# Encoder layer with a top-4-of-32 expert stage: halves of the gate/up loads, 128 stationary columns, bias on row groups

## The chip, the core and the metric

The kernel runs on one core of a Trainium2 chip. Five engines work beside each other: TensorE (PE, matrix products; PEld is its loading of the stationary operand), VectorE (DVE), ScalarE (ACT), GpSimd (POOL) and SyncE (SP), which issues most transfers. The sixteen DMA engines move data between the chip's memory and the core's buffer SBUF; TensorE writes into the eight banks of PSUM, each 128 partitions by 512 fp32. The metric is the time of one execution on the device in microseconds; the number compared is the median of several.

## What is computed

One layer of an encoder on 512 rows of 1024: three kinds of attention, a gated merge, and then an expert stage, on which the change lies. Cut to that:

```python
logits = ht @ w_router + b_router            # 512 rows, 32 experts
top_v, top_i = lax.top_k(logits, 4); gate = softmax(top_v)
# each of the 4 x 512 (row, expert) pairs goes to a block of its expert
def expert_block(args):
    xb, e = args
    gu = xb @ w_gu[e] + b_gu[e]              # 1024 x 2048, fp32
    g = jnp.minimum(gu[:, :D_EXPERT], SWIGLU_LIMIT)
    lin = jnp.clip(gu[:, D_EXPERT:], -SWIGLU_LIMIT, SWIGLU_LIMIT)
    act = g * jax.nn.sigmoid(SWIGLU_ALPHA * g) * (lin + 1.0)
    return act @ w_down[e] + b_down[e]       # 1024 x 1024, fp32
x = x + sum of gate * expert_block rows;  return rmsnorm(x, norm_final)
```

## The kernel before

The first 440 us hold the attention, the merge and the router, as 18 weight units of 512 columns. The rest is the expert stage. It works through jobs: a job is up to 96 rows (SLOTS) of one expert. There are 32 jobs with these inputs.

Products are near fp32. Each operand is split into a high part that TensorE takes in one pass (fp32r) and a low part, the rest. A product is high x high, high x low and low x high.

**Parts.** The weights of a job come as 12 parts of 1 MB, each 128 partitions by 2048 fp32: eight parts of the first matrix (gate/up, one chunk k of 128 input features each) and four of the second (down, two chunks each). A gate/up part has rows of 8192 bytes, a down part two rows of 4096 bytes per partition. They land in 12 slots `a_w` in turn. ScalarE copies part m into one of 8 slots `h_w` (the high part, `moe_high`), eight parts ahead of TensorE; VectorE writes the low part `l_w` over `a_w` (`moe_low`), seven ahead. TensorE finishes a part and adds 1 to `gemm_ps`; this frees the `h_w` slot for ScalarE and the `a_w` slot for SyncE, which then issues the load of the part twelve later (`load_gu` L591, `load_dn` L594, each one DMA that adds 16 to the slot's semaphore `part_in`). `wait_raw` waits for it.

**TensorE.** `gate_up` (L1731) first puts the bias into banks 0 to 3: four matmuls (L1735) with the stationary operand `expert_gu`, 96 x 96, and the moving operand `bias_gu`, the biases of all 32 experts in bf16 three times, as high, middle and low part on 3 x 32 partitions. Then for each part k: eight matmuls (L1743) with `xt_hi` and `xt_lo` (the job's rows, transposed, chunk k, 128 x 96) on `h_w`, and four (L1746) with `xt_hi` on `l_w`. Results stand on PSUM partitions 0 to 95. `down` (L1750) does the same with `at_hi`, `at_lo` into banks 4 and 5 (L1761, L1766). Eight transposes (`turn`, L1467) stand after part 1 of gate/up (the activated rows of the job before) and after part 0 of down (the rows of a later job). In the loop a pass has gate/up of job j+1 and then down of job j. The order on each engine is the order of the code, and engines meet at semaphores.

At the end, `down_biases` (L1810, its matmuls L1814) uses the bias of down on groups of 32 partitions, in plain fp32.

**Others.** GpSimd prepares `bias_gu` (L940 to L960), gathers a job's rows (`xg`, indirect DMA L971) and adds finished rows into `x_rows` (L976). ScalarE writes `expert_gu` for each job by broadcasting a column of `job_hot_b` (`name_gu`).

Of the kernel before, what the change touches and what calls it, by code (L numbers as in the profile page):

```python
# [102 lines left out]
def encoder_kernel(nc, x, mem, norm_mix, w_in, q_norm_a, k_norm_a, sink_b, norm_mem, w_mem_kv,  # L103
# [3 lines left out]
    with ctx:  # L107
# [40 lines left out]
        bias_f = sb("bias_f", [96, D], F32, 188 * KIB)  # L148
# [49 lines left out]
        bias_gu = sb("bias_gu", [96, 2 * D], BF16, 202 * KIB)  # L198
# [27 lines left out]
        blocks_end = small("blocks_end", [P, 3, N_EXP], F32)  # L226
        blocks_start = small("blocks_start", [P, 3, N_EXP], F32)
        job_ge = small("job_ge", [96, NJ], F32)
        job_lt = small("job_lt", [96, NJ], F32)
        job_hot = small("job_hot", [96, NJ], F32)  # L230
# [26 lines left out]
        at_hi = sb("at_hi", [P, KD, SLOTS], F32R, 174 * KIB)  # L257
        at_lo = sb("at_lo", [P, KD, SLOTS], F32R, 177 * KIB)
# [16 lines left out]
        job_hot_b = small("job_hot_b", [96, NJ], BF16)  # L275
        expert_gu = small("expert_gu", [96, SLOTS], BF16)
# [253 lines left out]
        def wait_raw(eng, i, m):  # L530
            eng.wait_ge(part_in[m % A_SLOTS], i * 32 + 16 * (m // A_SLOTS + 1))
# [13 lines left out]
        def _(sp):  # L545
# [44 lines left out]
            def load_gu(e, m, k):  # L590
                sp.dma_start(a_w[m % A_SLOTS][:], wgu[e, :, k, :]).then_inc(part_in[m % A_SLOTS], 16)  # L591
# [63 lines left out]
        def _(act):  # L655
# [157 lines left out]
            def moe_high(i, m):  # L813
                wait_raw(act, i, m)
# [22 lines left out]
            def name_gu(j):  # L837

                nc.scalar.activation(expert_gu[:], job_hot_b[:, bass.ds(j, 1)].to_broadcast([96, SLOTS]), ACT.Copy).then_inc(expert_gu_ready, 1)

            def take_xt(j):
                act.wait_ge(x_ps, j + 1)
                nc.scalar.activation(xt_hi[:].rearrange("p (h k) m -> p h (k m)", h=2), of_two_banks(6), ACT.Copy).then_inc(xt_hi_done, 1)

            def take_act(j):
                act.wait_ge(at_ps, j + 1)
                nc.scalar.activation(at_hi[:].rearrange("p (h k) m -> p h (k m)", h=2), of_two_banks(6), ACT.Copy).then_inc(at_hi_done, 1)
# [60 lines left out]
            for p in range(KD):  # L908
# [5 lines left out]
                moe_high(pairs_but_one, stream(0, p) + H_LEAD)  # L914
# [19 lines left out]
        def _(pool):  # L934
# [6 lines left out]
            bias_pieces = [(bias_gu[:, 0:D], b_gate_up[0][:, 0:D]), (bias_gu[:, D:2 * D], b_gate_up[0][:, D:2 * D])]  # L941
            pool.wait_ge(y_ps, STEPS)
            for n, (part, bias) in enumerate(bias_pieces):
                for g in range(3):
                    pool.dma_start(bias_f[N_EXP * g:N_EXP * (g + 1), :], bias).then_inc(bias_in, 16)
                pool.wait_ge(bias_in, 48 * (n + 1))

                def to_parts(rows):
                    step.link(nc.gpsimd.tensor_copy(part[rows, :], bias_f[rows, :]))

                def take_off(rows):
                    step.link(nc.gpsimd.tensor_tensor(bias_f[rows, :], bias_f[rows, :], part[rows, :], ALU.subtract))

                to_parts(slice(0, 96))
                for lo in (32, 64):
                    take_off(slice(lo, lo + 32))
                    to_parts(slice(lo, lo + 32))
                take_off(slice(64, 96))
                to_parts(slice(64, 96))
# [32 lines left out]
            step.link(nc.gpsimd.memset(expert_gu[:], 0.0))  # L992
            for g in range(3):
                nc.gpsimd.memset(expert_gu[N_EXP * g:N_EXP * g + 1, :], 1.0).then_inc(first_expert, 1)
            pool.wait_ge(first_expert, 3)
# [49 lines left out]
        def _(dve):  # L1045
# [227 lines left out]
            for g in range(3):  # L1273
                step.inc(nc.vector.tensor_tensor_scan(blocks_end[:, g, :], ones[:, 0:N_EXP], blocks[:], 0.0, ALU.mult, ALU.add))
            dve.wait_ge(dve_chain, step.n)
            for g in range(3):
# [4 lines left out]
            dve.wait_ge(blocks_ready, 3)  # L1281
# [4 lines left out]
            step.inc(nc.vector.tensor_tensor(job_ge[:], counter[0:96, 0:NJ], ps[0:96, 1, P:P + NJ], ALU.is_ge))  # L1286
            step.link(nc.vector.tensor_tensor(job_lt[:], counter[0:96, 0:NJ], ps[0:96, 1, 0:NJ], ALU.is_lt))
# [39 lines left out]
            def low_xt(j):  # L1327
                dve.wait_ge(xt_hi_done, j + 1)
                nc.vector.tensor_tensor(xt_lo[:].rearrange("p (h k) m -> p h (k m)", h=2), ps[:, 6:8, 0:4 * SLOTS],  # L1329
                                        xt_hi[:].bitcast(F32).rearrange("p (h k) m -> p h (k m)", h=2), ALU.subtract).then_inc(xt_lo_done, 1)  # L1330

            def low_act(j):
                dve.wait_ge(at_hi_done, j + 1)
                nc.vector.tensor_tensor(at_lo[:].rearrange("p (h k) m -> p h (k m)", h=2), ps[:, 6:8, 0:4 * SLOTS],
                                        at_hi[:].bitcast(F32).rearrange("p (h k) m -> p h (k m)", h=2), ALU.subtract).then_inc(at_lo_done, 1)
# [101 lines left out]
        def _(pe):  # L1437
# [264 lines left out]
            pe.wait_ge(blocks_ready, 3)  # L1702
# [27 lines left out]

            def gate_up(i, j, m0, between):  # L1731
# [129 lines left out]
```

## Time and profile before

| | us |
|---|---|
| median of 3 runs (1602.7 to 1605.66) | 1604.47 |
| the profiled execution | 1600.28 |
| its span | 1598.4 |
| PE busy in the span | 1566.0 |
| DVE busy | 1283.4 |
| ACT busy | 1084.7 |
| POOL busy | 432.0 |

The profile is of one execution, and its times are from the start of its span. Busy time of TensorE overstates it, since matmuls are pipelined and their ends are modelled; the starts are better to count with. "Chain" is the work that ended last, followed back from the end. The DMA share is the mean busy share of 16 engines and can pass 1 where packets overlap. 466.97 MB were moved in all.

### The profile page before, as it was taken

Reading aid. Unit: us, or ns where it says so; the run is one execution under the profiler, and the core shown is the slowest. Engines: PE = TensorE matmul, PEld = TensorE weight load, DVE = VectorE, ACT = ScalarE, POOL = GpSimd, SP = SyncE. Lnnn points to the kernel's source line nnn. Section 1 sums busy time; section 2 is a strip of 40 time slices with the busy share of each in tenths; the row PEclk is TensorE's granted clock in tenths of the full one; section 3 lists DMA queues with packets and bytes.
Section 4 is the critical chain, followed back from the end, with each engine's and each line's share of the span. In section 5 each row is a group of like instructions: output and inputs, shape, how many; then the busy total and the mean of one; then the engine's idle time right before and its main releaser. Section 6 shows DMA issues by size and latency. Waiting matters only on the chain.

```text
span 1598.4 us, 21810 instructions
## 1 busy us (share of the span) xinstructions
PE 1566.0 (98%) x7654; PEld 1139.1 (71%) x7654; DVE 1283.4 (80%) x1019; ACT 1084.7 (68%) x999; POOL 432.0 (27%) x265
## 2 busy tenths in 40 slices
PE   8999999999899999999999999999999999999997
PEld 7866688888766777777777777777777777777774
DVE  3768734337699989999898899998988999999984
ACT  6368723224477778777777787777777877777772
POOL 0000260000033622324432222344332223443220
PEclk9999999999999999999999999999999999999999
DMA  7310022337399999999999999999999999999983
GB/s 270 111 59 21 11 86 84 128 119 290 122 381 346 365 367 379 368 369 376 358 369 370 370 381 368 372 369 360 367 369 372 363 377 368 368 363 373 375 298 125
DMA packets 102566, 466.97 MB, mean 292 GB/s; under 512 B 13289, under 2 KB 13825, under 8 KB 69729
## 3 DMA queue, kind: packets, MB, share of 16 engines
q1 hardware_dynamic: 94416, 448.71, 73.5%
q0 software_dynamic: 7776, 17.68, 5.2%
q8 instruction: 24, 0.39, 0.1%
q10 hardware_dynamic: 336, 0.08, 0.0%
q14 instruction: 14, 0.11, 0.0%
HBM read 456.82 MB, written 19.27 MB: 298 GB/s over the span
## 4 chain that ended last, share of the span: by engine, by line
PE 91%; DVE 6%; issue 1%; DMA 1%; ACT 0%; POOL 0%; DVEq 0%; ACTq 0%; POOLq 0%
PE ps L1743 28%; PE ps L1761 14%; PE ps L1746 14%; PE ps L1766 7%; PE ps L1440 6%; PE ps L1442 6%; PE ps L1441 6%; PE ps L1467 4%; DVE l_w L1190 2%; PE ps L1735 2%; PE ps L1593 1%; DVE head_max L1119 1%; PE ps L1549 1%; DVE probs L1137 1%; PE ps L1476 0%
## 5 line engine op out<-in xcount | busy, mean ns | idle before, releaser
L1190 DVE TENSOR_TENSOR l_w<-a_w,h_w 128x2048 fp32r<-128x2048 f32 x384 | 865.4, 2290 | 31.0 <-ACT h_w L817 29.1
L817 ACT ACTIVATE h_w<-a_w 128x2048 fp32r<-128x2048 f32 x384 | 731.1, 1914 | 234.5 <-PE ps L1746 169.2
L965 POOL TENSOR_TENSOR mark_sb<-ones 1x1 f32<-1x1 f32 x93 | 245.9, 2644 | 718.6 <-ACT y_sb L865 708.5
L1743 PE MATMUL ps<-h_w,xt_hi 128*96 128x512 f32 x1024 | 286.7, 401 | 2.3 <-DVE xt_lo L1329 2.3
L1743 PE MATMUL ps<-h_w,xt_lo 128*96 128x512 f32 x1024 | 278.3, 393 | 0.0
L1746 PE MATMUL ps<-l_w,xt_hi 128*96 128x512 f32 x1024 | 277.9, 393 | 0.0
L1743 PEld LDWEIGHTS ps<-h_w,xt_lo 128*96 128x96 f32 x1024 | 165.6, 162 | 71.5
L1746 PEld LDWEIGHTS ps<-l_w,xt_hi 128*96 128x96 f32 x1024 | 165.2, 161 | 71.1
L1743 PEld LDWEIGHTS ps<-h_w,xt_hi 128*96 128x96 f32 x1024 | 163.3, 162 | 70.6 <-ACT h_w L817 1.7
L1761 PE MATMUL ps<-h_w,at_hi 128*96 128x512 f32 x512 | 162.1, 398 | 0.2 <-issue 0.2
L1761 PE MATMUL ps<-h_w,at_lo 128*96 128x512 f32 x512 | 159.5, 392 | 0.0
L486 DVE TENSOR_TENSOR w_low<-w_raw,w_high 128x2048 fp32r<-128x2048 f32 (+2 forms) x36 | 69.0, 1953 | 112.0 <-ACT w_high L478 112.0
L1766 PE MATMUL ps<-l_w,at_hi 128*96 128x512 f32 x512 | 139.0, 393 | 0.0
L1440 PE MATMUL ps<-w_high,h_hi 128*128 128x512 f32 x352 | 138.1, 392 | 0.6 <-DVE mem_lo L1065 0.5
L1442 PE MATMUL ps<-w_high,h_lo 128*128 128x512 f32 x352 | 137.1, 390 | 0.0
L1441 PE MATMUL ps<-w_low,h_hi 128*128 128x512 f32 x352 | 137.0, 389 | 0.0
L1761 PEld LDWEIGHTS ps<-h_w,at_lo 128*96 128x96 f32 x512 | 82.6, 161 | 36.1
L1766 PEld LDWEIGHTS ps<-l_w,at_hi 128*96 128x96 f32 x512 | 82.6, 161 | 35.9
L1761 PEld LDWEIGHTS ps<-h_w,at_hi 128*96 128x96 f32 x512 | 80.2, 162 | 32.1 <-issue 1.0
L971 POOL DMA_INDIRECT xg<-h_rows,gather_row x32 | 88.0, 2749 | 7.1 <-issue 5.4
L785 ACT ACTIVATE gate_sb<-ps,row_rstd 128x512 f32<-128x512 f32 x24 | 16.6, 690 | 105.7 <-PE ps L1442 105.7
L1440 PEld LDWEIGHTS ps<-w_high,h_hi 128*128 128x128 f32 x352 | 66.1, 188 | 15.1 <-DVE mem_lo L1065 0.8
(247 smaller groups left out, 1555.6 us busy)
## 6 DMA issues: line engine op xcount, KB each, us to landing
a_w<-in_w_gate_up SPq DMA_DIRECT2D x256, 1024.0 KB, 7.0
a_w<-in_w_down SPq DMA_DIRECT2D x128, 1024.0 KB, 6.6
w_raw<-in_w_in SPq DMA_DIRECT2D x8, 2048.0 KB, 8.0
w_raw<-in_w_out SPq DMA_DIRECT2D x2, 2048.0 KB, 7.6
w_raw<-in_w_in SPq DMA_DIRECT2D x2, 1024.0 KB, 7.8
x_sb<-in_x SPq DMA_DIRECT2D x8, 256.0 KB, 7.3
w_raw<-in_w_mem_kv SPq DMA_DIRECT2D x1, 2048.0 KB, 11.2
x<-in_x SPq DMA_DIRECT2D x4, 512.0 KB, 5.2
```

Of the source, the lines that this page charges most:

```text
L486: nc.vector.tensor_tensor(wl[u % 2][:, a * COLS:b * COLS], raw[u % 2][:, a * COLS:b * COLS], wh[u % 2][:, a * COLS:b * COLS].bitcast(F32), ...
L817: nc.scalar.activation(h_w[m % H_SLOTS][:], a_w[m % A_SLOTS][:], ACT.Copy).then_inc(wh_done, 1)
L965: nc.gpsimd.tensor_tensor(mark_sb[:], ones[0:1, 0:1], ones[0:1, 0:1], ALU.mult).then_inc(marked, 1)
L971: nc.gpsimd.indirect_dma_start(out=xg[s][:], out_offset=None, in_=h2_rows, in_offset=bass.IndirectOffsetOnAxis(ap=rows, axis=0), bounds_ch ...
L1190: nc.vector.tensor_tensor(l_w[m % A_SLOTS][:], a_w[m % A_SLOTS][:], h_w[m % H_SLOTS][:].bitcast(F32), ALU.subtract).then_inc(wl_done, 1)
L1440: nc.tensor.matmul(bank, hi, w_hi, start=start, stop=False)
L1441: nc.tensor.matmul(bank, hi, w_lo, start=False, stop=False)
L1442: return nc.tensor.matmul(bank, lo, w_hi, start=False, stop=stop)
L1743: nc.tensor.matmul(ps[0:SLOTS, n, :], x_part[:, k, :], w_h[:, n * COLS:(n + 1) * COLS], start=False, stop=False)
L1746: last = nc.tensor.matmul(ps[0:SLOTS, n, :], xt_hi[:, k, :], w_l[:, n * COLS:(n + 1) * COLS], start=False, stop=k == KD - 1)
L1761: nc.tensor.matmul(ps[0:SLOTS, 4 + n, :], a_part[:, 2 * q + k, :], w_h[:, (2 * k + n) * COLS:(2 * k + n + 1) * COLS], start=q == 0 and k = ...
L1766: last = nc.tensor.matmul(ps[0:SLOTS, 4 + n, :], at_hi[:, 2 * q + k, :], w_l[:, (2 * k + n) * COLS:(2 * k + n + 1) * COLS], start=False, s ...
```

## The change

- `load_gu` issues two DMAs per gate/up part, one for each half of the columns (rows of 4096 bytes). Both add 16 to the same semaphore; `landings` counts 32 for a gate/up part and 16 for a down part, and `wait_raw` waits for the sum.
- The stationary operand has 128 columns instead of 96. `xt` and `at_both` hold high and low part in a row, and `chunk` takes 128 columns from the start of a chunk of 96: the last 32 belong to the next chunk, and PSUM partitions 96 to 127 get values that nobody reads. The last chunk of the low part has nothing behind it and keeps 96 columns.
- The bias is split in two fp32r parts, `bias_hi` and `bias_lo`, with columns n x 512 to n x 512 + 511 on partitions 32 n to 32 n + 31. Each of the eight matmuls takes one group of 32 partitions and writes one bank, the four of `bias_hi` first. `expert_gu` is 128 x 128 in fp32r.
- GpSimd's preparation and some router tables follow these shapes (four copies instead of three).

```diff
-        bias_gu = sb("bias_gu", [96, 2 * D], BF16, 202 * KIB)
+        bias_hi = sb("bias_hi", [P, COLS], F32R, 202 * KIB)
+        bias_lo = sb("bias_lo", [P, COLS], F32R, 204 * KIB)
...
-        xt_hi = sb("xt_hi", [P, KD, SLOTS], F32R, 160 * KIB)
-        xt_lo = sb("xt_lo", [P, KD, SLOTS], F32R, 163 * KIB)
+        xt = sb("xt", [P, 2, KD * SLOTS], F32R, 160 * KIB)
+        xt_hi, xt_lo = (xt[:, n, :].rearrange("p (k m) -> p k m", k=KD) for n in range(2))
...
-        job_hot_b = small("job_hot_b", [96, NJ], BF16)
-        expert_gu = small("expert_gu", [96, SLOTS], BF16)
+        job_hot_b = small("job_hot_b", [P, NJ], F32)
+        expert_gu = small("expert_gu", [P, P], F32R)
...
+        def landings(m):
+
+            of_gate_up = m < KD or (m - KD) % PARTS < KD
+            return 32 if of_gate_up else 16
+
+        def wait_raw(eng, i, m, last_down=False):
+            once = sum(landings(n) for n in range(m % A_SLOTS, m, A_SLOTS)) + (16 if last_down else landings(m))
+            again = 0 if isinstance(i, int) else 2 * landings(m)
+            eng.wait_ge(part_in[m % A_SLOTS], i * again + once)
...
             def load_gu(e, m, k):
-                sp.dma_start(a_w[m % A_SLOTS][:], wgu[e, :, k, :]).then_inc(part_in[m % A_SLOTS], 16)
+                for n in range(2):
+                    half = slice(n * D, (n + 1) * D)
+                    sp.dma_start(a_w[m % A_SLOTS][:, half], wgu[e, :, k, half]).then_inc(part_in[m % A_SLOTS], 16)
...
-            bias_pieces = [(bias_gu[:, 0:D], b_gate_up[0][:, 0:D]), (bias_gu[:, D:2 * D], b_gate_up[0][:, D:2 * D])]
             pool.wait_ge(y_ps, STEPS)
...
+            for n in range(4):
+                pool.dma_start(bias_f[N_EXP * n:N_EXP * (n + 1), :], b_gate_up[0][:, n * COLS:(n + 1) * COLS]).then_inc(bias_in, 16)
+            pool.wait_ge(bias_in, 64)
+            step.link(nc.gpsimd.tensor_copy(bias_hi[:], bias_f[:]))
+            step.link(nc.gpsimd.tensor_tensor(bias_lo[:], bias_f[:], bias_hi[:].bitcast(F32), ALU.subtract))
...
-            step.link(nc.gpsimd.memset(expert_gu[:], 0.0))
-            for g in range(3):
-                nc.gpsimd.memset(expert_gu[N_EXP * g:N_EXP * g + 1, :], 1.0).then_inc(first_expert, 1)
-            pool.wait_ge(first_expert, 3)
+            step.link(nc.gpsimd.memset(expert_gu[:].bitcast(F32), 0.0))
+            for n in range(4):
+                nc.gpsimd.memset(expert_gu[N_EXP * n:N_EXP * n + 1, :].bitcast(F32), 1.0).then_inc(first_expert, 1)
+            pool.wait_ge(first_expert, 4)
...
+            def chunk(both, part, k):
+
+                w = SLOTS if part and k == KD - 1 else P
+                at = (part * KD + k) * SLOTS
+                return both[:].rearrange("p a m -> p (a m)")[:, at:at + w], w
+
             def gate_up(i, j, m0, between):

                 pe.wait_ge(expert_gu_ready, j + 1)
-                for n in range(4):
-                    nc.tensor.matmul(ps[0:SLOTS, n, :], expert_gu[:], bias_gu[:, n * COLS:(n + 1) * COLS], start=True, stop=False)
+                for part in (bias_hi, bias_lo):
+                    for n in range(4):
+                        rows = slice(N_EXP * n, N_EXP * (n + 1))
+                        nc.tensor.matmul(ps[:, n, :], expert_gu[rows, :], part[rows, :], start=part is bias_hi, stop=False)
...
-                    for x_part in (xt_hi, xt_lo):
+                    for part in range(2):
+                        x_part, rows = chunk(xt, part, k)
                         for n in range(4):
-                            nc.tensor.matmul(ps[0:SLOTS, n, :], x_part[:, k, :], w_h[:, n * COLS:(n + 1) * COLS], start=False, stop=False)
+                            nc.tensor.matmul(ps[0:rows, n, :], x_part, w_h[:, n * COLS:(n + 1) * COLS], start=False, stop=False)
```

On TensorE, in the loop, at the start of a gate/up product. `bias_gu`, `bias_hi` and `bias_lo` are moving operands, and `h_w`, `l_w` with a number are slots. Before:

```order
L1735 MATMUL ps<-bias_gu,expert_gu 96x512 [waits expert_gu_ready]
L1735 MATMUL ps<-bias_gu,expert_gu 96x512 x3
L534 ISA [waits xt_lo_done]
L1743 MATMUL ps<-h_w_176,xt_hi 96x512 [waits wh_done]
L1743 MATMUL ps<-h_w_176,xt_hi 96x512 x3
L1743 MATMUL ps<-h_w_176,xt_lo 96x512 x4
L1746 MATMUL ps<-l_w_172,xt_hi 96x512 [waits wl_done]
```

Now, at the same place:

```order
L1740 MATMUL ps<-bias_hi,expert_gu 128x512 [waits expert_gu_ready]
L1740 MATMUL ps<-bias_hi,expert_gu 128x512 x3
L1740 MATMUL ps<-bias_lo,expert_gu 128x512 x4
L542 ISA [waits xt_lo_done]
L1749 MATMUL ps<-h_w_177,xt 128x512 [waits wh_done]
L1749 MATMUL ps<-h_w_177,xt 128x512 x7
L1752 MATMUL ps<-l_w_173,xt 128x512 [waits wl_done]
```

Four more matmuls stand ahead of the wait for the low part of the rows; the others keep their places, and their results have 128 rows instead of 96.

On SyncE, the loads of the first gate/up part of the loop and the wait of the next. Before:

```order
L591 ISA [waits gemm_ps]
L591 DMA a_w_160<-in_w_gate_up 128x2048
L540 REGISTER_ALU
L591 ISA [waits gemm_ps]
L591 DMA a_w_161<-in_w_gate_up 128x2048
```

Now:

```order
L601 ISA [waits gemm_ps]
L601 DMA a_w_161<-in_w_gate_up 128x1024
L601 ISA
L601 DMA a_w_161<-in_w_gate_up 128x1024
L548 REGISTER_ALU
L601 ISA [waits gemm_ps]
L601 DMA a_w_162<-in_w_gate_up 128x1024
```

Each wait on `gemm_ps` now has two transfers of half the size behind it (the slot's number differs by one because the tiles are counted anew).

## Rows read from the trace of the kernel before

**Rows 1.** The page: the chain that ended last, by engine.

```profile
PE 91%; DVE 6%; issue 1%; DMA 1%; ACT 0%; POOL 0%; DVEq 0%; ACTq 0%; POOLq 0%
```

**Rows 2.** Chain, one job (928.91 to 964.37): start us, us, what.

```profile
928.91 0.87 PE ps L1735 x4
929.78 1.84 PE ps L1743 x8
931.62 0.92 PE ps L1746 x4
...
955.38 0.66 PE ps L1467 x8
...
964.37 0.87 PE ps L1735 x4
```

**Rows 3.** Chain, where TensorE takes it over, and after the last down product.

```profile
504.03 2.08 PE ps L1743 x8
...
1580.61 1.91 PE ps L1814 x4
```

**Rows 4.** Waits of the SyncE queue, 520 to 1520: us in total, times, longest.

```profile
SPq L591 <- PE ps L1746: 500.0, 226, 2.8
```

**Rows 5.** Window of one job: us, busy (x) of PE, PEld, DVE, ACT, POOL; PEclk, DMA share, GB/s.

```profile
929.37:964.82 35.45, 35.45 (x165) 25.01 (x164) 32.06 (x18) 27.59 (x20) 11.82 (x7) 1.00 1.00 372
```

**Rows 6.** Chain, 128-column matmuls of the projections, first and last of 142.

```profile
254.99 0.23 PE ps L1441
...
286.95 0.23 PE ps L1441
```

**Rows 7.** Window without DMA in the last job, and chain there, 96 columns.

```profile
1561.51:1566.80 5.29, 5.29 (x29) 3.86 (x28) 2.04 (x1) 0.00 (x0) 0.00 (x0) 1.00 0.01 2
...
1560.97 1.85 PE ps L1761 x8
1562.83 0.93 PE ps L1766 x4
```

**Rows 8.** Chain, 128 columns, second, 11th and 20th matmul after transposes.

```profile
21.94 0.23 PE ps L1441
...
24.03 0.23 PE ps L1441
...
26.07 0.23 PE ps L1441
```

**Rows 9.** The page, part 5: loads of 96 and of 128 stationary columns.

```profile
L1743 PEld LDWEIGHTS ps<-h_w,xt_lo 128*96 128x96 f32 x1024 | 165.6, 162 | 71.5
...
L1440 PEld LDWEIGHTS ps<-w_high,h_hi 128*128 128x128 f32 x352 | 66.1, 188 | 15.1 <-DVE mem_lo L1065 0.8
```

**Rows 10.** Chain at the down bias, then PE's timeline at the scores.

```profile
1567.20 1.92 PE ps L1814 x8
...
1569.27 2.09 PE ps L1761 x8
...
112.99 1.13 PE L1549 MATMUL ps<-k_t,q_t 64*128 64x512 f32 x4
114.05 1.09 PE L1467 MATMUL ps<-ident,probs 128*128 128x128 f32 x8
```

**Rows 11.** SyncE's issues of gate/up parts, 504 to 1540: ns min/median/max.

```profile
L591 SPq DMA_DIRECT2D a_w<-in_w_gate_up x232: 333/333/349, 507.2 to 1520.1; - x116
```

**Rows 12.** Windows with 2048-byte rows and with 8192-byte rows, columns as in rows 5.

```profile
10.00:15.00 5.00, 5.00 (x38) 4.74 (x37) 2.73 (x4) 2.37 (x4) 0.00 (x0) 1.00 1.05 395
...
445.00:450.00 5.00, 5.00 (x25) 3.54 (x24) 5.00 (x2) 3.52 (x2) 1.40 (x1) 1.00 1.01 426
```

**Rows 13.** Landings of gate/up loads issued at 908.9 and at 932.7.

```profile
DMA to landing us min/median/max: 8.1/8.1/8.1
...
DMA to landing us min/median/max: 4.7/4.7/4.7
```

**Rows 14.** Timeline of GpSimd before the first gather.

```profile
427.32 0.62 POOL L994 MEMSET expert_gu<- 1x96 bf16 x3
```

More of the change, by code:

```diff
@@ L251, in encoder_kernel @@
         h_w = [sb(f"h_w{i}", [P, 2 * D], F32R, at * KIB) for i, at in enumerate((0, 8, 16, 24, 128, 136, 112, 120))]
[L254 to L255 removed]
+        xt = sb("xt", [P, 2, KD * SLOTS], F32R, 160 * KIB)
+        xt_hi, xt_lo = (xt[:, n, :].rearrange("p (k m) -> p k m", k=KD) for n in range(2))
         xg = [sb(f"xg{i}", [SLOTS, D], F32, (166 + 4 * i) * KIB) for i in range(2)]
[L257 to L258 removed]
+        at_both = sb("at_both", [P, 2, KD * SLOTS], F32R, 174 * KIB)
+        at_hi, at_lo = (at_both[:, n, :].rearrange("p (k m) -> p k m", k=KD) for n in range(2))
         sg_sb = sb("sg_sb", [SLOTS, D], F32, 180 * KIB)
@@ L1272, in _ @@
             step.link(nc.vector.tensor_scalar(blocks[:, 0:1], blocks[:, 0:1], 1.0, None, ALU.max))
-            for g in range(3):
+            for g in range(TB):
                 step.inc(nc.vector.tensor_tensor_scan(blocks_end[:, g, :], ones[:, 0:N_EXP], blocks[:], 0.0, ALU.mult, ALU.add))
             dve.wait_ge(dve_chain, step.n)
-            for g in range(3):
+            for g in range(TB):
                 nc.vector.tensor_tensor(blocks_start[:, g, :], blocks_end[:, g, :], blocks[:], ALU.subtract).then_inc(blocks_ready, 1)
             step.inc(nc.vector.tensor_scalar(job_table[0:1, 1, 1:2], blocks_end[0:1, 0, N_EXP - 1:N_EXP], 0.5, -0.75, ALU.mult, ALU.add))
-            dve.wait_ge(blocks_ready, 3)
+            dve.wait_ge(blocks_ready, TB)
             step.link(nc.vector.scalar_tensor_tensor(out=place[:], in0=blocks_start[:, 0:1, :].to_broadcast([P, TB, N_EXP]), scalar=float(SLOTS),
@@ L1740, in gate_up @@
                     wait_high(pe, i, m)
-                    for x_part in (xt_hi, xt_lo):
+                    for part in range(2):
+                        x_part, rows = chunk(xt, part, k)
                         for n in range(4):
-                            nc.tensor.matmul(ps[0:SLOTS, n, :], x_part[:, k, :], w_h[:, n * COLS:(n + 1) * COLS], start=False, stop=False)
+                            nc.tensor.matmul(ps[0:rows, n, :], x_part, w_h[:, n * COLS:(n + 1) * COLS], start=False, stop=False)
                     wait_low(pe, i, m)
                     for n in range(4):
-                        last = nc.tensor.matmul(ps[0:SLOTS, n, :], xt_hi[:, k, :], w_l[:, n * COLS:(n + 1) * COLS], start=False, stop=k == KD - 1)
+                        last = nc.tensor.matmul(ps[:, n, :], chunk(xt, 0, k)[0], w_l[:, n * COLS:(n + 1) * COLS], start=False, stop=k == KD - 1)
                     last.then_inc(gemm_ps, 1)
@@ L1758, in down @@
                     for k in range(2):
-                        for a_part in (at_hi, at_lo):
+                        for part in range(2):
+                            a_part, rows = chunk(at_both, part, 2 * q + k)
                             for n in range(2):
-                                nc.tensor.matmul(ps[0:SLOTS, 4 + n, :], a_part[:, 2 * q + k, :], w_h[:, (2 * k + n) * COLS:(2 * k + n + 1) * COLS],
-                                                 start=q == 0 and k == 0 and a_part is at_hi, stop=False)
+                                nc.tensor.matmul(ps[0:rows, 4 + n, :], a_part, w_h[:, (2 * k + n) * COLS:(2 * k + n + 1) * COLS],
+                                                 start=q == 0 and k == 0 and part == 0, stop=False)
                     wait_low(pe, i, m)
@@ L1765, in down @@
                         for n in range(2):
-                            last = nc.tensor.matmul(ps[0:SLOTS, 4 + n, :], at_hi[:, 2 * q + k, :], w_l[:, (2 * k + n) * COLS:(2 * k + n + 1) * COLS],
+                            last = nc.tensor.matmul(ps[:, 4 + n, :], chunk(at_both, 0, 2 * q + k)[0], w_l[:, (2 * k + n) * COLS:(2 * k + n + 1) * COLS],
                                                     start=False, stop=q == DN_PARTS - 1 and k == 1)
```

54 lines of the change are left out of this document (19 added, 35 removed).

## The prediction

> **What bounds the kernel now.** I read the page first, then the chain of waits over one job of the expert stage, then the waits of the SyncE queue, then the windows. The chain that ended last is 91% TensorE [rows 1], but 98% busy of TensorE would not prove it, since ends of matmuls are modelled. The chain shows it: from one bias (L1735) to the next, 928.91 to 964.37 us, every piece is TensorE and none is a wait; a job takes 35.46 us, and a part of the weights (8 matmuls with h_w, 4 with l_w) 1.84 + 0.92 us [rows 2]. TensorE takes the chain over from VectorE at 504.03 us [rows 3]. Before that point the stage is still catching up behind VectorE's splits, so what TensorE saves before 504 us gains nothing. From there to the end of the last down product (1580.61 us) lie 30 gate/up products and 31 down products. The SyncE queue waits for it, 500.0 us in all, for free slots [rows 4]. In one job VectorE is busy 32.06 of 35.45 us and ScalarE 27.59, but the DMA engines' share is 1.00 at 372 GB/s [rows 5]. So there is about 3.4 us of room on VectorE, and perhaps none on DMA.
>
> The sum is made against the profiled execution, 1600.28 us with a span of 1598.4; the median of the runs shown is 1604.47, 0.26% above. I subtract the saving from the median.
>
> **Part 1, 128 columns in the stationary operand.** The count of the main matmuls stays: 96 in a gate/up product, 48 in a down product. What counts is the step from start to start. Before, a job has 35.46 - 0.87 (bias) - 2 x 0.66 (transposes) = 33.27 us for 144 matmuls, 231.0 ns each [rows 2]. The projections have the same matmul with 128 columns: from 254.99 to 286.95 us lie 141 of them, 226.7 ns each [rows 6]. The difference is 4.4 ns. DMA traffic is not its cause: in the last job, with a DMA share of 0.01, 12 matmuls of 96 columns still took 2.78 us, 231.7 ns each [rows 7]. But 128 columns do not give 226.7 at once. After the transposes at 20 to 21.5 us, the nine matmuls from 21.94 to 24.03 us took 232 ns each, and only the next nine 226.7 [rows 8]. It is as if the pipeline has to settle after a break. A job has five breaks: two groups of transposes, the bias, and the two places where 96 columns remain (the low part of chunk 7, 4 matmuls in gate/up and 2 in down, which must not read past the tile). I take nine unsettled matmuls after each, 45, plus the 6 themselves: 93 of 144 are settled, 93 x 4.4 = 0.41 us per job. If none of it settles the gain is 0; if all 138 do, 0.60 us.
>
> Loading 128 columns takes 188 ns against 162 [rows 9]. Inside a run of matmuls this is hidden, since 188 is under the step of 227; after a break the first load is exposed, 26 ns at three breaks, 0.08 us per job.
>
> The Trainium skill, "TensorE: Matmul & The Clock Gate", section "LDWEIGHTS (loading the stationary operand)", speaks against this change: a load costs its columns / 1.2 ns, so 32 columns more cost 27 ns. The trace agrees on the size (26 ns). Were each load exposed, the job would be 144 x 27 ns = 3.9 us slower; the rows of the projections show that it is hidden.
>
> **Part 2, the bias.** Removed: 4 matmuls in bf16 over 96 rows, 0.87 us in the chain [rows 2]. Added: 8 over 32 rows each, on four different row groups and four banks, high parts first. The nearest row is the down bias (L1814), also 32 rows by 128 columns between full-width matmuls. There 8 passes over two row groups take 1.92 us, and 4 passes on a single row group 1.91 us, so two row groups do run side by side [rows 3, 10]. A pass of this plain fp32 product is about 0.43 us: at the scores (L1549, 64 rows) two rounds of two passes take 1.06 us with all around them [rows 10]. After its end at 1569.12 us come 0.16 us of nothing up to 1569.27, and then eight matmuls that take 2.09 us where 1.85 is usual. Four rounds of 0.43 are 1.71, so entering and leaving the 32-row form cost 1.92 + 0.16 + 0.24 - 1.71 = 0.61 us. The scores give less: 1.06 us for two rounds, 0.21 us over. An fp32r pass streams once where plain fp32 streams at half that rate: about 0.21 us. With four groups side by side the bias costs 2 x 0.21 + 0.61 = 1.03 us, +0.16 per job; with the overhead of the scores 0.63, -0.24. I take +0.10, nearer to L1814, whose form and surroundings are those of the new bias. Four groups at once is not shown by any row; if only two overlap, it is 0.42 us more per job, and if none do, 1.26.
>
> The Trainium skill, "TensorEngine Tiling", section "Key Properties", states that a change of tiling mode drains TensorE. The 0.61 us of L1814 agrees with it; the page gives no price.
>
> **Part 3, two transfers of half rows.** Same bytes; 8 of a job's 12 loads become 16 of 512 KB. SyncE spends 0.33 us to issue one [rows 11]; two in a part's 2.76 us fit, and both sit behind the same wait on its queue, so nothing else is held up by more than 0.33 us. ScalarE now waits for both halves, and the second is issued 0.33 us later. On the DMA engines the price is the row. With 8192-byte rows a window moved 426 GB/s at a share of 1.01, with 2048-byte rows 395 at 1.05 [rows 12]: 311 and 87 ns per row and engine, so on a straight line 162 for 4096 bytes, 13 ns more per 8192. A job has 8 loads of 8 such rows on each of 16 engines: 64 x 13 = 0.83 us of DMA time. What hides it is slack between issue and need. A load is issued when TensorE frees its slot and is needed by ScalarE four parts later, 11.1 us. A landing took 8.1 us at its worst in a job and 4.7 at the best [rows 13], so the queue does run nearly empty once per job. I charge 0.
>
> **Part 4, the rest.** GpSimd's preparation of the bias gets shorter (4 loads and 2 operations for 6 and 12), far off the chain. Before the first gather it sets one row more and a larger tile: three rows took 0.62 us [rows 14], so about +0.25 us once, on the chain. One scan, one subtraction and a wider copy of the expert's column vanish beside TensorE.
>
> **Sum.** Per job -0.41 + 0.08 + 0.10 = -0.23 us; 30 jobs, -6.9; the last down product has no bias, -0.1; start +0.25. About -6.8 us: profiled 1593.5, median 1597.7, 0.4% faster.
>
> **Rivals.**
> A. The settled step comes at once everywhere and leaving the row groups is cheap: -0.60 - 0.1 per job, -21 us, 1583.5. For: stretches of over a hundred matmuls at 226.7. Against: the slow nine after a break. More likely half of it, about 1590.
> B. DMA becomes the bound. If the share of 1.00 is real work, a job needs 35.46 + 0.83 = 36.3 us and the whole run is 30 x 0.83 = 25 us slower, 1629; it decides as soon as the landings pass 11 us and ScalarE waits for a_w. Against: landings fall to 4.7 us in each job, and a share above 1 (1.05 in one window) shows that the share overstates. With part of it, 0.3 us per job over now, 1613. This is the case on the other side.
> The Trainium skill, "DMA: Bandwidth & Descriptors", section "Rules for kernel authors", asks for at least 1 MiB per DMA, so it would side with B; no run here shows 512 KB transfers in a row yet.
> C. The row groups overlap only in twos: -0.23 + 0.42 = +0.19 per job, +6, 1610; with none, +1.03 per job, +31, 1635.
> D. The split does not do what it says: alternating banks or waits inside each part, not the columns, give 231 ns. Then 0 + 0.08 + 0.10 per job, +5.6, 1610.
>
> **How the numbers follow.** Differences within 0.2% (3.2 us) are about what a measurement of this kernel can tell from no change. Forecast 0.47 (0.40 faster, 0.07 same; own range 1592 to 1602); A 0.14, faster; B 0.13 (0.03 faster, 0.03 same, 0.07 slower); C 0.14 (0.04 same, 0.10 slower); D 0.12 (0.04 same, 0.08 slower). Faster 0.57, same 0.18, slower 0.25. The range runs from the half of A to the milder B: 1587 to 1613.
>
> **What would show it.** Right: in the chain of a job the eight matmuls with h_w take 1.81 to 1.82 us in most parts instead of 1.84, the bias about 1.0 us, the job 35.2, landings of the halves stay under 10 us and no ScalarE wait on a_w appears. Wrong: parts still at 1.84 (D), the bias at 1.4 or more (C), a wait of ScalarE or VectorE for the transfer of a_w and a job over 35.5 (B), a job under 34.9 (A).

## The result

| | before | after |
|---|---|---|
| median of 7 runs each | 1603.7 (1602.42 to 1605.66) | 1608.63 (1605.8 to 1611.17) |
| the profiled execution, its span | 1600.28, 1598.4 | 1605.8, 1603.9 |

The ratio is 1.003, 95% interval 1.0019 to 1.0042: slower by 0.3%. The forecast was 1597.7, faster; the time lies inside the range (1587 to 1613), but on the other side of no change.

The page of the changed kernel: busy time, the chain by engine, and the gate/up loads (KB each, median us to landing).

```profile
PE 1570.6 (98%) x7782; PEld 1248.9 (78%) x7782; DVE 1278.7 (80%) x1021; ACT 1085.7 (68%) x999; POOL 394.6 (25%) x252
...
PE 92%; DVE 5%; issue 1%; DMA 1%; ACT 0%; POOL 0%; DVEq 0%; ACTq 0%; POOLq 0%
...
a_w<-in_w_gate_up SPq DMA_DIRECT2D x512, 512.0 KB, 6.9
```

TensorE still sets the end, and it loads its operands longer (1248.9 us for weight loads, 1139.1 before). Now one job in the chain of the changed kernel, from bias to bias. L1740 is the bias, L1749 and L1752 the gate/up matmuls on `h_w` and `l_w`, L1768 and L1773 those of down.

```profile
931.03 0.67 PE ps L1740 x5
931.70 2.04 PE ps L1749 x8
933.74 0.91 PE ps L1752 x4
934.65 1.87 PE ps L1749 x8
936.52 0.93 PE ps L1752 x4
...
943.70 1.84 PE ps L1749 x8
945.54 0.91 PE ps L1752 x4
...
961.08 1.86 PE ps L1768 x8
962.94 0.93 PE ps L1773 x4
...
966.67 0.67 PE ps L1740 x5
```

Against [rows 2] the reader sees three things. The job takes 966.67 - 931.03 = 35.64 us where it took 35.46; 30 jobs make 5.4 us, and the spans differ by 5.5. So nearly the whole loss lies in the period of the job. The two spans can be compared, since in both executions TensorE takes over the chain at the same time (504.03 us [rows 3] and 503.94); in other executions it is up to 3.4 us later, for a reason given at the kernel with chunks 512 bytes apart. Bias and first eight matmuls together take 0.67 + 2.04 = 2.71 us, as before (0.87 + 1.84 [rows 2]). And the parts come in two kinds: away from a break, a part with an even chunk k takes 1.84 + 0.91 us, one with an odd chunk 1.87 + 0.93. Not one part reaches 1.81. No piece of the job is a wait.

The chain of the kernel before has the same two kinds, closer together, which I passed over when I predicted: 1.84 us with k = 4 and 1.85 with k = 5, and so on through the job.

```profile
941.53 1.84 PE ps L1743 x8
...
944.29 1.85 PE ps L1743 x8
```

The job's period is the number to compare in all that follows. From start to start of the bias it is the same for job after job within 0.02 us (0.04 in the kernels with chunks 512 bytes apart), so that differences of 0.01 us can be read where the medians can't tell 2 us.

### The profile page after: what moved, and what is told of

Its sections match the earlier page's. It is cut to its first block, busy times and chain, and to the rows that moved or that the text cites. A ratio compares the mean times of both kernels' runs of the same rounds, so it can differ in the third digit from the quotient of the medians.

```text
span 1603.9 us, 22838 instructions
## 1 busy us (share of the span) xinstructions
PE 1570.6 (98%) x7782; PEld 1248.9 (78%) x7782; DVE 1278.7 (80%) x1021; ACT 1085.7 (68%) x999; POOL 394.6 (25%) x252
## 4 chain that ended last, share of the span: by engine, by line
PE 92%; DVE 5%; issue 1%; DMA 1%; ACT 0%; POOL 0%; DVEq 0%; ACTq 0%; POOLq 0%
PE ps L1749 29%; PE ps L1768 14%; PE ps L1752 14%; PE ps L1773 7%; PE ps L1437 6%; PE ps L1439 6%; PE ps L1438 6%; PE ps L1464 4%; DVE l_w L1187 2%; PE ps L1740 1%; PE ps L1590 1%; DVE head_max L1116 1%; PE ps L1546 1%; DVE probs L1134 1%; PE ps L1667 0%
## 5 line engine op out<-in xcount | busy, mean ns | idle before, releaser
L1749 PE MATMUL ps<-h_w,xt 128*128 128x512 f32 (+1 forms) x2048 | 523.5, 397 | 2.8 <-DVE xt L1326 2.8
L1749 PEld LDWEIGHTS ps<-h_w,xt 128*128 128x128 f32 (+1 forms) x2048 | 377.6, 187 | 101.6 <-issue 11.3
L1752 PE MATMUL ps<-l_w,xt 128*128 128x512 f32 x1024 | 277.5, 393 | 0.0
L1768 PE MATMUL ps<-h_w,at_both 128*128 128x512 f32 (+1 forms) x1024 | 261.4, 397 | 0.2 <-issue 0.2
L1752 PEld LDWEIGHTS ps<-l_w,xt 128*128 128x128 f32 x1024 | 192.7, 188 | 43.8
L1768 PEld LDWEIGHTS ps<-h_w,at_both 128*128 128x128 f32 (+1 forms) x1024 | 188.6, 187 | 44.8 <-issue 1.0
L1773 PE MATMUL ps<-l_w,at_both 128*128 128x512 f32 x512 | 140.8, 397 | 0.0
L1773 PEld LDWEIGHTS ps<-l_w,at_both 128*128 128x128 f32 x512 | 96.4, 188 | 23.5
L1439 PEld LDWEIGHTS ps<-w_high,h_lo 128*128 128x128 f32 x352 | 66.1, 188 | 13.9
L1438 PEld LDWEIGHTS ps<-w_low,h_hi 128*128 128x128 f32 x352 | 66.1, 188 | 13.2
```

Source lines behind the costliest of these rows:

```text
L1438: nc.tensor.matmul(bank, hi, w_lo, start=False, stop=False)
L1439: return nc.tensor.matmul(bank, lo, w_hi, start=False, stop=stop)
L1749: nc.tensor.matmul(ps[0:rows, n, :], x_part, w_h[:, n * COLS:(n + 1) * COLS], start=False, stop=False)
L1752: last = nc.tensor.matmul(ps[:, n, :], chunk(xt, 0, k)[0], w_l[:, n * COLS:(n + 1) * COLS], start=False, stop=k == KD - 1)
L1768: nc.tensor.matmul(ps[0:rows, 4 + n, :], a_part, w_h[:, (2 * k + n) * COLS:(2 * k + n + 1) * COLS], start=q == 0 and k == 0 and part == 0, ...
L1773: last = nc.tensor.matmul(ps[:, 4 + n, :], chunk(at_both, 0, 2 * q + k)[0], w_l[:, (2 * k + n) * COLS:(2 * k + n + 1) * COLS], start=False ...
```

## Experiments: which part of the change costs

Four kernels, each one part of the change, measured beside each other. First, **only the two transfers**, the rest as before:

```
-                sp.dma_start(a_w[m % A_SLOTS][:], wgu[e, :, k, :]).then_inc(part_in[m % A_SLOTS], 16)
+                for n in range(2):
+                    half = slice(n * D, (n + 1) * D)
+                    sp.dma_start(a_w[m % A_SLOTS][:, half], wgu[e, :, k, half]).then_inc(part_in[m % A_SLOTS], 16)
```

> The kernel before with the gate/up loads as two halves and nothing else. Theory T (all of the 180 ns per job lies on TensorE, in the steps of the matmuls): a job stays at 35.46 us, the run within 0.1% of before. Rival R (the halves cost DMA time that reaches TensorE, 0.83 us per job at most): a job at 35.6 us or more, the run 4 us or more slower, and a wait of ScalarE for a_w in the trace.

Median 1602.67 us, ratio 0.9995 (0.9985 to 1.0005). Two biases in its chain, 35.46 us apart, exactly the job of before:

```profile
932.28 0.86 PE ps L1744 x4
...
967.74 0.86 PE ps L1744 x4
```

**Only the columns** (`xt`, `at_both`, `chunk` and the main matmuls of the change, whole loads, and the bf16 bias with 128 columns):

```
-        expert_gu = small("expert_gu", [96, SLOTS], BF16)
+        expert_gu = small("expert_gu", [96, P], BF16)
...
-                    nc.tensor.matmul(ps[0:SLOTS, n, :], expert_gu[:], bias_gu[:, n * COLS:(n + 1) * COLS], start=True, stop=False)
+                    nc.tensor.matmul(ps[:, n, :], expert_gu[:], bias_gu[:, n * COLS:(n + 1) * COLS], start=True, stop=False)
```

> The kernel before with 128 stationary columns (as in the changed kernel, also with the six matmuls of 96 left in) and with the bf16 bias over 96 rows, its stationary operand widened to 128 columns; whole loads. T: a job takes 35.64 us as in the changed kernel, because the first matmuls of each part run at 232 ns and up, and some at 241, and only the last five of a gate/up part at 226.7; run about 5.5 us slower than before. R: 35.46 or less.

Median 1608.6 us, ratio 1.0032 (1.0022 to 1.0042), the whole loss. In its chain the job takes 969.17 - 933.53 = 35.64 us (35.633 on average):

```profile
933.53 0.88 PE ps L1741 x4
934.41 1.83 PE ps L1750 x8
...
969.17 0.88 PE ps L1741 x4
```

**Only the bias** on row groups, with 96 columns everywhere and whole loads (the edit is against the kernel with the whole change):

```
-                w = SLOTS if part and k == KD - 1 else P
+                w = SLOTS
...
-                        nc.tensor.matmul(ps[:, n, :], expert_gu[rows, :], part[rows, :], start=part is bias_hi, stop=False)
+                        nc.tensor.matmul(ps[0:SLOTS, n, :], expert_gu[rows, 0:SLOTS], part[rows, :], start=part is bias_hi, stop=False)
```

> The changed kernel with whole loads and with 96 stationary columns everywhere: only the bias on row groups is left. T: from the last matmul of down to the second of gate/up 1.33 us both before and after, so a job takes 35.46 us (35.44 to 35.48), the run as before. Rival (entering and leaving the row groups costs 0.1 to 0.2 us): 35.56 to 35.66.

Median 1602.76 us, ratio 0.9996 (0.9986 to 1.0006), job 966.04 - 930.64 = 35.40 us, below both values expected. Bias and the first eight matmuls take 0.64 + 2.01 = 2.65 us, 0.06 less than before:

```profile
930.64 0.64 PE ps L1731 x7
931.28 2.01 PE ps L1740 x8
...
966.04 0.64 PE ps L1731 x7
```

**The change with whole loads** (columns and bias together), against the changed kernel:

```
-                for n in range(2):
-                    half = slice(n * D, (n + 1) * D)
-                    sp.dma_start(a_w[m % A_SLOTS][:, half], wgu[e, :, k, half]).then_inc(part_in[m % A_SLOTS], 16)
+                sp.dma_start(a_w[m % A_SLOTS][:], wgu[e, :, k, :]).then_inc(part_in[m % A_SLOTS], 16)
```

> The changed kernel with the loads undone: one transfer of 8192-byte rows per gate/up part. T: a job stays at 35.64 us, the run as the changed kernel's, about 5 us over before. R (the halves are what costs): a job at 35.46 or less, the run no slower than before.

Median 1609.34 us, ratio 1.0039 (1.0027 to 1.005), job 35.64 us as in the changed kernel. So the transfers do nothing, the bias gains 0.06 us a job at 96 columns and nothing at 128, and 32 more columns cost 0.17 us beside the bf16 bias (35.46 to 35.63) and 0.24 beside the row groups (35.40 to 35.64), where a gain of 0.33 was forecast.

## Experiments: why 128 columns don't settle

My rival D said that waits or banks inside each part hold the step at 231 ns. The bank order can't be taken out without another kernel, the waits can. **One wait for four parts** (against the change with whole loads; TensorE waits for `h_w` and `l_w` together, once, for the last of four parts, and the same in down):

```
-                    wait_high(pe, i, m)
+                    if isinstance(i, int):
+                        wait_high(pe, i, m)
+                        wait_low(pe, i, m)
+                    elif k % 4 == 0:
+                        wait_high(pe, i, m + 3)
+                        wait_low(pe, i, m + 3)
```

> The changed kernel (128 columns, bias on row groups, whole loads) in which TensorE waits once for four parts, ahead of the first of them, instead of twice in each part; the counts of finished parts stay. Theory W (the wait and its register instructions at the head of each part unsettle the steps, eight matmuls each time): the steps of 226.7 ns now run on over the heads of parts without a wait, and a job takes about 35.3 us instead of 35.64. Rival I (not the waits, but what the matmuls themselves do at the head of a part: the stationary operand taken again four times, the banks, the count at its end): the same steps of 232 and 241 ns at every head, 35.64 us.

One time, 1615.66 us, but that is the start: its last 30 jobs begin 8.7 us later than with whole loads alone (513.1 against 504.4 us), 7.0 of them in the second job. Theory W had a job of 35.3 us. The job is the same to 0.01 us, 940.90 to 976.54 = 35.64:

```profile
940.90 0.67 PE ps L1731 x5
...
976.54 0.67 PE ps L1731 x5
```

The same edit with 96 columns and the bf16 bias:

> The kernel before with the same single wait for four parts, 96 columns. W: less jitter, a job at 35.3 us or less and the run 4 us or more faster. I: 35.46 us and the run within 0.1% of before. If waiting early for four parts costs anything, a wait of TensorE for VectorE's l_w appears at the head of a group.

Median 1609.57 us (ratio 1.0034, 1.0015 to 1.0054), again with a later start, and a job of 35.46 us as before. Neither expectation had that later start. The waits are not it: this half of D's cause falls.

**No operand of 96 columns left** (`full128`; the last chunk of the low part starts 32 columns early, so its matmuls compute something else):

```
-                w = SLOTS if part and k == KD - 1 else P
-                at = (part * KD + k) * SLOTS
+                w = P
+                at = min((part * KD + k) * SLOTS, 2 * KD * SLOTS - P)
```

> The changed kernel with whole loads in which the last low chunk has 128 columns too. It takes them 32 columns early, so the contribution of that chunk is shifted by 32 rows and wrong; the amount of work is that of 128 columns everywhere. Theory (the six matmuls of 96 are only six of many breaks): a job within 0.05 us of 35.64. Rival (the mixture of 96 and 128 is what costs the 0.24 us): 35.4 us or less.

One time, 1609.2 us; the job takes 35.67 us (35.66 and 35.68 in turn), 0.03 more and not less. So the six matmuls of 96 columns are not what this layout loses by. Nor do nine slow ones follow them: in the changed kernel only the four matmuls on `l_w` stand between those of gate/up and the first steps of down, and the first three of these are already 226 or 227 ns. **64 columns** in all matmuls but the first and last of each accumulation (`cols64`, bf16 bias):

```
-                w = SLOTS if part and k == KD - 1 else P
+                w = SLOTS if full else 64
```

> The kernel before with 64 stationary columns in the main matmuls, except for the first and the last of each accumulation, which keep 96; rows 64 to 95 of each job are left without most of their sum. It measures the step at a third point. If the time of a load of the stationary operand sets the step at the breaks (162 ns at 96 columns, 188 at 128), the step falls below 231.0 ns on average, to about 227, and a job to about 34.9 us. If columns below 96 no longer matter: 35.46 us.

One time, 1602.5 us, job 967.14 - 931.71 = 35.43 us, near the 35.46 of the second expectation and far from 34.9. So fewer columns, whose loads are shorter, gain 0.03 us: on this layout the step does not follow the length of the load.

What did follow a pattern were the parts of even and odd k. Chunk k of `xt` starts 384 k bytes into its partition, so even chunks start at multiples of 256 bytes and odd ones 128 bytes past one. A part of down takes one chunk of each. In the projections, where 226.7 ns was read [rows 6], the stationary operand `hi[:, k, m]` always starts at a multiple of 512 bytes. The steps of all jobs, worked out from the starts of the matmuls (without those at a break, some 1250 in each cell), say the same:

| kernel | even k: mean ns, settled | odd k | down |
|---|---|---|---|
| before, 96 columns | 230.1, 0% | 231.6, 0% | 231.2, 2% |
| after, 128 columns | 229.6, 39% | 232.8, 0% | 233.2, 9% |

Settled is a step of 226 or 227 ns. In the changed kernel 15% of the steps of odd parts and 16% of down's are 240 or 241 ns, a length that before has nowhere.

**Chunks 512 bytes apart.** If the start address decides, the change is worth what I thought, on another layout. `PITCH` is 128 columns, the 32 columns between the chunks are zeroed once, and the copies into `xt` and `at_both` skip them:

```
-        xt = sb("xt", [P, 2, KD * SLOTS], F32R, 160 * KIB)
-        xt_hi, xt_lo = (xt[:, n, :].rearrange("p (k m) -> p k m", k=KD) for n in range(2))
+        xt = sb("xt", [P, 2, KD * PITCH], F32R, 160 * KIB)
+        xt_hi, xt_lo = (xt[:, n, :].rearrange("p (k m) -> p k m", k=KD)[:, :, 0:SLOTS] for n in range(2))
...
-                w = SLOTS if part and k == KD - 1 else P
-                at = (part * KD + k) * SLOTS
+                w = P
+                at = (part * KD + k) * PITCH
```

> The changed kernel with whole loads, and the chunks of xt and at laid 128 columns (512 bytes) apart instead of 96 (384 bytes), so that each of 128 columns starts on a multiple of 512 bytes and no place with 96 is left (the 32 columns between hold zeros; y_sb and others moved by some KiB for it). Theory A (in gate/up only the parts with even k reach steps of 226.7 ns, and their chunk starts on a multiple of 768 bytes, the odd ones 384 further: the start address of the stationary operand is what counts): all parts settle within some seven matmuls of a break and a job takes about 35.0 us. Rival B (the order of matmuls, same operand four times over four banks, unsettles it): odd parts still without a step of 226.7, 35.64 us.

Median 1589.45 us (1586.93 to 1593.66), ratio 0.9923 (0.99 to 0.9946), faster than both kernels. Its chain:

```profile
926.48 0.67 PE ps L1734 x7
...
936.25 1.81 PE ps L1743 x8
938.06 0.91 PE ps L1746 x4
938.97 1.81 PE ps L1743 x8
940.78 0.91 PE ps L1746 x4
...
953.23 1.88 PE ps L1762 x8
955.11 0.92 PE ps L1767 x4
956.03 1.81 PE ps L1762 x8
...
961.47 0.68 PE ps L1734 x7
```

Every part away from a break takes 1.81 + 0.91 us, odd and even alike, and the job 35.00 us (34.99, 35.00 and 35.03 in turn). Of the steps of odd parts, of even parts and of down, 100, 82 and 80% are settled; the rest are the nine or ten behind the bias and behind the transposes in down. TensorE takes over the chain at 507.05 us:

```profile
507.05 2.09 PE ps L1743 x8
```

That is 3.0 us later than before [rows 3]. 30 jobs x 0.455 us - 3.0 = 10.6 us, and the span is 10.8 us shorter.

The later start is not the layout's. The windows from 423 to 429 us (columns as in [rows 5]) have TensorE's granted clock at 1.00 in the trace of before, at 0.61 in that of `halves_only` and at 0.50, its lower level of 1.2 GHz, in this one:

```profile
423.00:429.00 6.00, 4.30 (x36) 3.73 (x34) 4.49 (x27) 5.99 (x12) 2.86 (x12) 1.00 0.22 87
...
423.00:429.00 6.00, 5.95 (x34) 5.76 (x34) 3.00 (x17) 5.99 (x12) 2.70 (x11) 0.61 0.22 87
...
423.00:429.00 6.00, 6.00 (x28) 6.00 (x29) 2.86 (x16) 5.97 (x12) 2.85 (x12) 0.50 0.22 87
```

The chain is taken over at 504.03, 507.39 and 507.05 us. `halves_only` has the old layout and the job of before, and its profiled execution is still 3.4 us longer:

```profile
507.39 2.08 PE ps L1752 x8
```

Nor is it GpSimd's zeroing: with 96 columns on the new layout nothing is zeroed, and the chain is taken over at 506.31 us. So about 3 us of a profiled span can belong to the execution and not to the kernel.

The same layout **with 96 columns**, main matmuls and bias:

```
-                w = P
+                w = SLOTS
```

> The same layout of 512 bytes per chunk with 96 stationary columns everywhere and the bias on row groups (whole loads): the count of columns alone differs from the other run. A in its strong form (address alone): steps settle here too, 35.0 us or less. A with the columns (both needed): 35.40 us, as with 96 columns in the old layout. B: 35.40.

Median 1598.19 us, ratio 0.9971 (0.9959 to 0.9982), job 965.87 - 930.59 = 35.28 us (35.273 on average), where 35.40 or 35.0 was expected:

```profile
930.59 0.63 PE ps L1732 x6
...
950.48 0.92 PE ps L1744 x4
951.39 1.84 PE ps L1741 x8
953.24 0.92 PE ps L1744 x4
...
965.87 0.63 PE ps L1732 x6
```

The steps are 230.0 ns in all three kinds of part, and none is settled. So the layout alone gains 0.13 us (odd chunks no longer take 231.5), but 226.7 ns needs both. The four jobs, all with whole loads and the bias on row groups:

| | 96 columns | 128 columns |
|---|---|---|
| chunks 384 bytes apart | 35.40 | 35.64 |
| chunks 512 bytes apart | 35.27 | 35.00 |

The same 32 columns cost 0.24 us on one layout and gain 0.27 on the other.

**The same distance, other starts.** The new layout changed three things: where chunks start, the 128 bytes between them, and what stands in columns 96 to 127. This kernel keeps the last two. Only `xt` begins 128 bytes later and `at_both` 256 bytes later (with what lies behind them):

```
-        xt = sb("xt", [P, 2, KD * PITCH], F32R, 160 * KIB)
+        xt = sb("xt", [P, 2, KD * PITCH], F32R, 160 * KIB + 128)
...
-        at_both = sb("at_both", [P, 2, KD * PITCH], F32R, 176 * KIB)
+        at_both = sb("at_both", [P, 2, KD * PITCH], F32R, 176 * KIB + 256)
```

> The kernel with 128 columns, row-group bias, whole loads and chunks 512 bytes apart (its job took 35.00 us, 12 steps of a settled part 1.81 + 0.91 us), with nothing changed but where the two operand buffers begin: xt 128 bytes later in each partition, at_both (and what lies behind it) 256 bytes later. Columns, data, zeroed gaps, the 512 bytes between chunks, loads and the order stay. Theory (the start address of the stationary operand decides whether the steps settle at 226.7 ns): the chunks of xt now all start 128 bytes past a multiple of 256, as the chunks with odd k did in the changed kernel, so the gate/up parts lose the settled steps: 8 pieces of 1.84 to 1.87 and 4 of 0.92 to 0.93 us, 0.04 to 0.07 us more a part and 0.3 to 0.55 us a job, so at least 35.3 us a job and 1598 us in all. The down parts tell how fine the grid is: if a multiple of 256 bytes is enough they stay at 1.81 and 0.91 us (job 35.3 to 35.55), if it takes 512 they go to 1.84 to 1.87 as well (job 35.45 to 35.75, 1603 to 1611 us). Rival (the gap of 128 bytes between the chunks, or the zeros in columns 96 to 127 in place of the next chunk's numbers, did it, and not the address): both kinds of part stay at 1.81 and 0.91 us, job 35.00, 1589.5 us.

Median 1604.35 us, ratio 1.0015 (1.0004 to 1.0025). Chain:

```profile
932.58 0.67 PE ps L1734 x7
...
945.29 1.86 PE ps L1743 x8
947.14 0.94 PE ps L1746 x4
...
962.63 1.81 PE ps L1762 x8
964.44 0.91 PE ps L1767 x4
...
968.07 0.68 PE ps L1734 x7
```

The gate/up parts, whose operand moved by 128 bytes, have lost the settled step: 1.86 + 0.94 us, 0% settled, 12 and 16% of the steps at 240 ns or more in even and odd parts. The down parts, moved by 256, kept it: 1.81 + 0.91, 79% settled. The job takes 35.49 us. One run thus holds both answers: the start of the stationary operand decides, not gap or data, and a multiple of 256 bytes is enough.

**The whole change on that layout**, with the two transfers as well (the edit of `halves_only`):

> The whole change (two transfers of 4096-byte rows, 128 columns, row-group bias) on the layout with chunks 512 bytes apart. The kernel beside it with whole loads took 1589.45 us, 35.00 us a job, while the DMA engines show a share of 0.99 to 1.00 there. Theory (the matmul steps set the job, the transfers hide whichever way they are cut, as with 96 and 128 columns on the old layout): job 35.00 us, 1589 to 1591 us, ratio 0.991 to 0.993. Rival (at a job shorter by 0.6 us the loads are the next limit, and rows of 4096 bytes take about 0.83 us more of the DMA engines' time a job, my term for the halves): waits of ScalarE on a_w appear, job 35.3 us or more, 1598 us or more.

Median 1591.12 us, ratio 0.993 (0.9914 to 0.9946), a job of 35.00 us. The landings of its halves issued from 504 to 1540 us, and then ScalarE's only wait for them between 520 and 1520 (us in total, times, longest):

```profile
DMA to landing us min/median/max: 4.3/7.1/11.5
```

```profile
ACT h_w L828 <- DMA a_w<-in_w_gate_up: 1.3, 2, 0.6
```

The slowest landing now passes the 11.1 us between issue and need, which shows as two short waits in 30 jobs, and TensorE doesn't feel them. With whole loads on this layout the slowest gate/up or down landing was 9.8 us and there was no such wait. The room is used up here. The intervals of this kernel and of the one with whole loads overlap.

## The prediction, step by step

**What bounds the kernel**: right. The chain of a job is TensorE alone in every kernel, and 30 jobs times the change of the period give the change of the span (5.4 of 5.5 us; 10.6 of 10.8).

**Part 1, the columns: this step failed.** Its sum was -0.41 us (93 of 144 matmuls settled, 4.4 ns each) + 0.08. Measured were +0.17 to +0.24. The wrong link is the transfer of 226.7 ns from [rows 6]. I compared two groups that differed in columns and named columns as the cause; they differed also in where the stationary operand starts, every 512 bytes there and every 384 bytes here, and I did not ask what else differed. Some 22 of the 136 steps away from breaks are settled (39% of 46, 0% of 46, 9% of 44), not 93, and some 14 are as long as 240 ns. By the table, even parts gain 46 x 0.5 = 0.02 us, odd parts lose 46 x 1.2 = 0.06 and down 44 x 2.0 = 0.09. The other 0.06 us of the 0.18 lie at the breaks. There the term for the exposed load was right in kind and size: from the first to the second matmul behind the transposes it took 289 and 292 ns before and 314 and 318 after, some 26 ns at two places a job.

The "nine matmuls behind a break" held where the operand starts well: ten behind the bias and nine or ten in down, none in gate/up behind the transposes. With aligned chunks columns give -0.40 us (35.40 to 35.00, layout and columns together), near the -0.33 that I had for this part. That it comes so near is in part luck: about 119 steps settled and not 93, and 0.13 of the 0.40 is the layout's own. What was right in the mechanism was worth nothing without its second condition. That the 96-column matmuls are further breaks is not borne out (`full128`).

The Trainium skill, "TensorE: Matmul & The Clock Gate", section "LDWEIGHTS (loading the stationary operand)", has the load grow with the columns; the trace agrees (162 ns in [rows 9], 187 to 188 after). Away from breaks the load is hidden: with it at 188 ns the step was still 226.7. The row of the load can't show the effect of the start either: in the changed kernel and in the one with chunks 512 bytes apart it is

```profile
L1749 PEld LDWEIGHTS ps<-h_w,xt 128*128 128x128 f32 (+1 forms) x2048 | 377.6, 187 | 101.6 <-issue 11.3 <-ACT h_w L827 2.0 <-DVE xt L1326 1.7
```

```profile
L1743 PEld LDWEIGHTS ps<-h_w,xt 128*128 128x128 f32 x2048 | 380.7, 188 | 90.9 <-issue 12.7
```

187 and 188 ns, with bad starts and good ones.

**Part 2, the bias**: the bounds held (-0.24 to +0.16), the value was off. I took +0.10; it was 0.00 with 128 columns and -0.06 with 96. What no row had shown is in TensorE's timeline of the changed kernel (start us, us):

```profile
930.63 0.40 PE L1773 MATMUL ps<-l_w,at_both 128*128 128x512 f32 x1
930.96 0.51 PE L1740 MATMUL ps<-bias_hi,expert_gu 32*128 32x512 f32 x4
931.30 0.40 PE L1740 MATMUL ps<-bias_lo,expert_gu 32*128 32x512 f32 x4
931.63 1.19 PE L1749 MATMUL ps<-h_w,xt 128*128 128x512 f32 x4
```

Four matmuls on four row groups start within 0.01 us of each other, so all four overlap, and rival C falls. A round takes 0.34 and 0.33 us, though, not the 0.21 that I had for the pass itself, while entering and leaving cost 0.1 us each (0.33 us from the last down matmul to the first round, and 0.33 from the first gate/up matmul to the second, where 0.23 is usual) and not 0.61 together. That makes 0.87 where I had 1.03 on that side of the bounds: two errors that partly cancel. The Trainium skill, "TensorEngine Tiling", section "Key Properties", says that a change of tiling drains the engine; those 0.1 us agree with it. The price of 0.61 us from L1814 [rows 10] didn't carry over. That product is plain fp32 and on two row groups; which of these makes the difference no run shows.

**Part 3, the two transfers**: right. Charged 0, measured 0.00 us a job. The slack I named is real, though smaller than I read it. The 8.1 us of [rows 13] was the slowest load of one job; over all jobs before it was 9.6. In the changed kernel landings took 4.1 to 10.1 us, under 11.1, and ScalarE never waited for `a_w`:

```profile
DMA to landing us min/median/max: 4.1/6.8/10.1
```

Rival B falls: halves of 512 KB gave 0.9995. The Trainium skill ("DMA: Bandwidth & Descriptors", section "Rules for kernel authors") asks for 1 MiB or more per DMA for the most bandwidth; in this kernel, where the landings are hidden, going below it cost nothing. The last kernel shows where a price would begin.

**Part 4, the start**: charged +0.25 us, measured none. GpSimd came to the zeros and rows ahead of the first gather earlier, and the gather starts no later than before (428.84 us there):

```profile
428.73 4.11 DMA xg<-h_rows,gather_row
```

**Rival D** had the outcome, 1610 for 1608.63, by a cause that isn't so: not waits, and the step did not stay at 231 but changed in both directions. Its +0.18 us (0 + 0.08 + 0.10) meets the measured 0.18 by accident: of it 0.12 us come from the steps and 0.06 from the breaks, and nothing from the bias. That 1608.63 lies inside the range is luck too: the upper end came from B, and B did not happen.

**Open.** Why the start matters I can't say; the load's record has the same length either way. Starts at 32, 64 or 192 bytes past a multiple of 256 were not tried, and I don't know why 96 columns stay at 230.0 ns at the best starts. Why the clock fell near 422 us in one execution and not in another is open too. The order of banks, the other half of D's cause, was not taken apart, but the settled parts use the same order, so it can't hold the step at 231.

## To carry to other kernels

When a faster step is read off one stage and expected in another, list everything in which the two operands differ (columns, start address, distance between slices, partitions) before naming a cause, and test it with one kernel. On this evidence, slices of a stationary fp32r operand of 128 columns (with 512 moving columns) should start at multiples of 256 bytes in their partition; here the layout alone gave a third of what both gave together, and the columns alone cost time. Where an engine's chain is one repeated period, measure the period: it separates 0.01 us where medians have an interval of 2 us. Before giving a difference of 3 us between two spans to a change, compare the granted clock in the stretches outside the period.

## What the hardware showed

- Of the layouts tried, a run of fp32r matmuls with 512 moving columns kept to a step of 226.7 ns only where the stationary operand had 128 columns and started at a multiple of 256 bytes; 128 bytes off, gate/up steps go from 226 to 242 ns (mean 232.2 to 232.8). With 96 columns they are 230.0 ns at multiples of 512 bytes, and 231.6 in the odd chunks before.
- So at a bad start 128 columns are worse than 96 (232.8 against 231.6), at a good one better (226.7 against 230.0).
- Four 32-row matmuls on four row groups and banks start within 0.01 us; a round takes 0.33 us, and changing to the row groups and back costs 0.1 us each.
- With the gate/up loads alone cut into 512 KB halves, these landed in 3.8 to 9.7 us, and the job kept its 35.46 us.
- Two executions with the same job of 35.46 us (before and `halves_only`) differ by 3.4 us in their spans; TensorE's granted clock from 423 to 429 us was 1.00 in one and 0.61 in the other.
